# A decoder layer on one Trainium2 core: the final RMSNorm moved from channels-on-partitions to tokens-on-partitions, with the last down projection reordered

## The chip, the cores and the metric

The kernel runs on one core of one Trainium2 chip. The metric is the device time of one execution in microseconds (us). The core has five engines with a program each: TensorE (PE in the profile, its weight loads PEld), VectorE (DVE), ScalarE (ACT), GpSimd (POOL), and SyncE (SP), which issues the DMAs. They meet at semaphores only.

## What is computed

One inference step of a hybrid causal decoder with one layer: 1024 prompt tokens and 8 sample tokens, each a row of 1024 channels (`D_MODEL`). The layer adds sparse attention with a conformer convolution, cross-attention, and a ConvFFN to the residual stream `x`. The last two statements are what this study is about:

```python
    up = rmsnorm(x, lw['norm_ffn']) @ lw['w_up']
    up_ext = jnp.concatenate([ffn_prev.astype(up.dtype), up], axis=1)
    g, val = jnp.split(causal_dwconv(up_ext, lw['ffn_dw'], lw['ffn_db']), 2, axis=-1)
    x = x + (jax.nn.silu(g) * val) @ lw['w_down']
...
def rmsnorm(x, g):
    xf = x.astype(jnp.float32)
    y = xf * lax.rsqrt(jnp.mean(xf * xf, -1, keepdims=True) + RMS_EPS)
    return (y * g.astype(jnp.float32)).astype(x.dtype)
...
    y_prompt = rmsnorm(yp, norm_final)
    y_sample = rmsnorm(ys, norm_final)
```

## The kernel before

The residual stream lies in SBUF as `xT`: channels on the 128 partitions, in 8 blocks (`KT` = 8), and the 1032 tokens (`T`) along the free axis, taken in three thirds of 344 columns (`CH`). Every product is made from three matmuls on high and low parts (`w_hi`, `w_lo`; `h_hi`, `h_lo`; `g_hi`, `g_lo`). The order of the work on each engine is written out by hand, with semaphore counts as the only link between engines.

The ConvFFN runs over 11 groups of hidden channels (`NG`). For each group PE makes the up projection of the next group (`up`) and then the down projection of this one (`down`): 24 units of 6 matmuls, one for each of 8 channel blocks `m` and 3 thirds `c`, with `c` inside. Each unit goes to one PSUM bank, and DVE adds it to `xT` (L1596). Semaphore `g_done` counts units, `res_c` counts the adds; PE may start a unit when the add that frees its bank is done.

The end of the program, after the last `down` (L2093), is the part that the change rewrites. Before the change it runs so:

- While the last down group runs, ACT squares each finished channel block of `xT` (`squares(3)`, L805), and DVE sums the squares over blocks into `n_rstd` (L1184, L1187), four blocks after the first 12 adds and four after the last.
- PE turns the last two up-projection columns (`upl`) by five transposes (L2097), for the small output `ffn_out`, and sums `n_rstd` over partitions by a matmul with ones (`norm_sum`, L1658).
- DVE and ACT make the reciprocal root for each of the three thirds (L1191, L1192, L814), and DVE writes the normalised `yT` in eight instructions (L1196).
- For each of nine token tiles (eight of 128 prompt tokens, one of the 8 sample tokens) PE makes eight 128x128 transposes of `yT` into a pair of PSUM banks (L2110), ACT copies one bank and DVE the other into the token-major buffer `y_tok` (L1169, L1618), and SP sends it out by one 512 KB DMA (L657). There are two `y_tok` buffers and two bank pairs.

A norm with tokens on partitions stands at the program's start too, on the input: ACT squares a row of 1024 with a running sum and takes the root (L768, L769), DVE takes the reciprocal and scales by it and by the gain, broadcast over partitions (L1219, L1224).

Of the kernel before, what the change touches and what calls it, by code (L numbers as in the profile page):

```python
# [20 lines left out]
ALU = mybir.AluOpType  # L21
# [3 lines left out]
P = 128  # L25
D = 1024
# [3 lines left out]
DB = 8  # L30
# [186 lines left out]
def build(nc, a, o):  # L217
# [27 lines left out]
    def sem(name):  # L245
        return ctx.enter_context(nc.semaphore(name))
# [184 lines left out]

    r = rz.again(out_at)
    fst = r.take("ffn_out", [2 * 2 * FT, 5, P])
    ytk = [r.take(f"y_tok{i}", [P, D]) for i in range(2)]
    yT = rh.again().take("yT", [P, KT, T])

# [53 lines left out]
    y_out = [sem(f"y_out{i}") for i in range(2)]  # L490

# [42 lines left out]
    def _(sp):  # L534
# [117 lines left out]

        for t in range(NB + 1):
            sp.wait_ge(yo_a, t + 1)
            sp.wait_ge(yo_d, t + 1)
            if t < NB:
                sp.dma_start(o["y_prompt"][0, t * P:(t + 1) * P, :], ytk[t % 2][:, :]).then_inc(y_out[t % 2], 16)  # L657
            else:
                sp.dma_start(o["y_sample"][:, 0, :], ytk[t % 2][0:DB, :]).then_inc(y_out[t % 2], 16)
        sp.wait_ge(y_out[0], 16 * 5)  # L660
        sp.wait_ge(y_out[1], 16 * 4)
        sp.wait_ge(ffn_out, 16 * (2 + DB))
# [96 lines left out]
    def _(act):  # L759
# [47 lines left out]
        def norm(i):  # L807

            if i < 3:
                squares(i)  # L810
# [351 lines left out]

        norm(3)
        for t in range(NB + 1):
            act.wait_ge(yo_t, 2 * t + 1)
            if t >= 2:
                act.wait_ge(y_out[t % 2], 16 * (t // 2))
            rows = P if t < NB else DB
            act.activation(ytk[t % 2][0:rows, 0:512], ps[0:rows, 3 + 2 * (t % 2), :], ACT.Copy).then_inc(yo_a, 1)  # L1169


    @block.vector
    def _(dve):
        self_ = Chain(dve, dve_self)

        def norm(i, gain, residual=None):
# [16 lines left out]
            dve.wait_ge(n_rstd, 3 * i)  # L1193
            if i == 3:
                for k in range(KT):
                    dve.scalar_tensor_tensor(out=yT[:, k, :], in0=xT[:, k, :], scalar=vec[:, gain + k:gain + k + 1],  # L1196
                                             in1=nr[:, :], op0=ALU.mult, op1=ALU.mult).then_inc(n_h, 1)
                return
            for k in range(KT):
# [411 lines left out]
        self_.n = n0 + 4 * (NG - 1)  # L1611
        norm(3, 32, lambda k: down(NG - 1, k // 4, UNITS_TO[SLOTS - 2]) if k % 4 == 0 else None)
        for t in range(NB + 1):
            dve.wait_ge(yo_t, 2 * t + 2)
            if t >= 2:
                dve.wait_ge(y_out[t % 2], 16 * (t // 2))
            rows = P if t < NB else DB
            dve.tensor_copy(ytk[t % 2][0:rows, 512:1024], ps[0:rows, 4 + 2 * (t % 2), :]).then_inc(yo_d, 1)  # L1618


    @block.tensor
    def _(pe):
# [470 lines left out]
        down(NG - 1, SLOTS - 2, (NG - 1) % 2, True)  # L2093
# [50 lines left out]
```

## Time and profile before

| | |
|---|---|
| median of 3 timed runs | 1976.29 us (1969.69 to 1976.4) |
| profiled execution, its own time | 1968.74 us |
| span of that execution, first to last instruction | 1966.9 us |
| PE busy / DVE busy / ACT busy / POOL busy | 85% / 59% / 31% / 28% of the span |
| mean granted TensorE clock | 0.914 of full speed |

The profile and all rows below are of the one profiled execution, which took 1968.74 us; 1.84 us of that lie outside its span. Two of the three timed runs are about 7.6 us above it, one is 1 us above it. A busy share is an average over stages; the end of the program is read by its own windows.

### The profile page before, as it was taken

Reading aid. Unit: us, or ns where it says so; the run is one execution under the profiler, and the core shown is the slowest. Engines: PE = TensorE matmul, PEld = TensorE weight load, DVE = VectorE, ACT = ScalarE, POOL = GpSimd, SP = SyncE. Lnnn points to the kernel's source line nnn. Section 1 sums busy time; section 2 is a strip of 40 time slices with the busy share of each in tenths; the row PEclk is TensorE's granted clock in tenths of the full one; section 3 lists DMA queues with packets and bytes.
Section 4 is the critical chain, followed back from the end, with each engine's and each line's share of the span. In section 5 each row is a group of like instructions: output and inputs, shape, how many; then the busy total and the mean of one; then the engine's idle time right before and its main releaser. Section 6 shows DMA issues by size and latency. Waiting matters only on the chain.

```text
span 1966.9 us, 28667 instructions
## 1 busy us (share of the span) xinstructions
PE 1668.8 (85%) x10229; PEld 1506.3 (77%) x10229; DVE 1158.0 (59%) x2001; ACT 606.9 (31%) x1235; POOL 547.7 (28%) x342
## 2 busy tenths in 40 slices
PE   6978696997898387799788699999999999999983
PEld 6966595995373155599677599989989999999983
DVE  5467898999975465524633746336346336336366
ACT  6344555311221464401341332202212202212212
POOL 1231232222000254323001153433433433433420
PEclk9999798997688599999886899999999999999996
DMA  7320021321442100041012011111111111111102
GB/s 228 84 58 24 22 75 56 85 75 25 121 146 86 64 1 1 1 140 32 11 40 78 22 54 43 44 44 43 44 44 43 44 44 43 44 44 44 43 15 91
DMA packets 138747, 110.63 MB, mean 56 GB/s; under 512 B 12324, under 2 KB 120092, under 8 KB 138354
## 3 DMA queue, kind: packets, MB, share of 16 engines
q1 hardware_dynamic: 128325, 102.19, 17.3%
q10 hardware_dynamic: 10301, 6.73, 1.1%
q8 instruction: 87, 1.43, 0.3%
q14 instruction: 34, 0.28, 0.0%
HBM read 93.56 MB, written 16.00 MB: 56 GB/s over the span
## 4 chain that ended last, share of the span: by engine, by line
PE 67%; DVE 16%; issue 7%; ACT 5%; DMA 2%; POOL 1%; SPq 1%; DVEq 1%; ACTq 0%; POOLq 0%
PE ps L1634 40%; PE ps L1688 10%; PE ps L1626 4%; DVE hits L1326 2%; PE ps L1649 2%; PE ps L1944 2%; PE ps L1893 2%; PE ps L1867 1%; DVE logits L1495 1%; DVE up_conv L1578 1%; DVE n_rstd L1192 1%; DVE sc L1285 1%; DVE n_rstd L1187 1%; DVE up_conv L1577 1%; DVE logits L1492 1%
## 5 line engine op out<-in xcount | busy, mean ns | idle before, releaser
L1634 PE MATMUL ps<-h_hi,w_hi 128*128 128x344 f32 x1200 | 385.1, 321 | 8.7 <-DVE xT L1596 4.6
L681 POOL TENSOR_SCALAR w_hi<-w_raw 128x1024 fp32r<-128x1024 f32 (+1 forms) x107 | 118.3, 1106 | 973.3 <-PE ps L1634 508.0
L1634 PE MATMUL ps<-h_lo,w_hi 128*128 128x344 f32 x1200 | 384.0, 320 | 0.0
L1634 PE MATMUL ps<-h_hi,w_lo 128*128 128x344 f32 x1200 | 383.9, 320 | 0.0
L683 POOL TENSOR_TENSOR w_lo<-w_raw,w_hi 128x1024 fp32r<-128x1024 f32 (+1 forms) x107 | 283.6, 2650 | 8.9
L1634 PEld LDWEIGHTS ps<-h_hi,w_hi 128*128 128x128 f32 x1200 | 225.9, 188 | 10.3 <-DVE xT L1596 5.7
L1577 DVE SCALAR_TENSOR_TENSOR up_conv<-up,fw,up_conv 128x1024 f32<-128x1024 f32 x44 | 72.9, 1657 | 263.7 <-ACT upl L1142 263.7
L1634 PEld LDWEIGHTS ps<-h_hi,w_lo 128*128 128x128 f32 x1200 | 226.1, 188 | 0.0
L1634 PEld LDWEIGHTS ps<-h_lo,w_hi 128*128 128x128 f32 x1200 | 226.0, 188 | 0.0
L1596 DVE TENSOR_TENSOR xT<-xT,ps 128x344 f32<-128x344 f32 x264 | 135.2, 512 | 147.4 <-PE ps L1634 144.2
L1634 PE MATMUL ps<-g_hi,w_hi 128*128 128x344 f32 x528 | 175.5, 332 | 36.1 <-DVE xT L1596 36.1
L1688 PE MATMUL ps<-h_hi,w_hi 128*128 128x344 f32 (+1 forms) x600 | 198.9, 331 | 2.9 <-ACTq L869 2.9
L1688 PE MATMUL ps<-h_lo,w_hi 128*128 128x344 f32 (+1 forms) x600 | 195.0, 325 | 0.0
L1688 PE MATMUL ps<-h_hi,w_lo 128*128 128x344 f32 (+1 forms) x600 | 194.9, 325 | 0.0
L1634 PE MATMUL ps<-g_lo,w_hi 128*128 128x344 f32 x528 | 174.4, 330 | 0.0
L1634 PE MATMUL ps<-g_hi,w_lo 128*128 128x344 f32 x528 | 174.0, 330 | 0.0
L1139 ACT ACTIVATE up<-ps 128x344 f32<-128x344 f32 x132 | 61.8, 468 | 350.0 <-POOL g_lo L754 238.6
L1399 DVE SCALAR_TENSOR_TENSOR ps<-u,cw,ps 128x512 f32<-128x512 f32 x232 | 153.2, 747 | 0.2 <-issue 0.2
L1634 PEld LDWEIGHTS ps<-g_hi,w_hi 128*128 128x128 f32 x528 | 104.1, 197 | 39.5 <-DVE xT L1596 38.5
L1688 PEld LDWEIGHTS ps<-h_hi,w_hi 128*128 128x128 f32 (+1 forms) x600 | 115.1, 192 | 9.4 <-issue 7.8
L1688 PEld LDWEIGHTS ps<-h_lo,w_hi 128*128 128x128 f32 (+1 forms) x600 | 114.8, 191 | 0.8
L1688 PEld LDWEIGHTS ps<-h_hi,w_lo 128*128 128x128 f32 (+1 forms) x600 | 114.5, 191 | 0.4
(338 smaller groups left out, 2900.2 us busy)
## 6 DMA issues: line engine op xcount, KB each, us to landing
w_raw<-in_w_up SPq DMA_DIRECT2D x44, 512.0 KB, 3.9
w_raw<-in_w_in SPq DMA_DIRECT2D x24, 512.0 KB, 3.9
w_raw<-in_w_down SPq DMA_DIRECT2D x22, 512.0 KB, 3.6
s_k_page<-in_cache_k SPq DMA_DIRECT2D x32, 256.0 KB, 2.8
s_v_pages<-in_cache_v SPq DMA_DIRECT2D x32, 256.0 KB, 2.9
xT<-x_spill SPq DMA_DIRECT2D x1, 4128.0 KB, 12.2
x_tok<-in_x_prompt SPq DMA_DIRECT2D x8, 512.0 KB, 7.8
x_spill<-x_raw SPq DMA_DIRECT2D x16, 256.0 KB, 2.8
```

The source lines that it names most:

```text
L681: pool.tensor_scalar(view(wh), view(wr), 1.0, 0.0, ALU.mult, ALU.add).then_inc(w_hi, 1)
L683: pool.tensor_tensor(view(wl), view(wr), view(wh).bitcast(F32), ALU.subtract).then_inc(w_lo, 1)
L1139: act.activation(e[:, 2 + c * CH:2 + (c + 1) * CH], src, ACT.Copy)
L1326: dve.tensor_scalar(hit(b), row(b), col(cand, b), col(below, b), ALU.is_lt, ALU.add, accum_out=col(cnt, b)).then_inc(th_cnt, 1)
L1399: dve.scalar_tensor_tensor(out=ps[:, 4 + e, :], in0=u[:, m, bass.ds(j + 512 * e, 512)], scalar=cw[:, bass.ds(CT * j + m, 1)], in1=ps[:, 4 ...
L1577: dve.scalar_tensor_tensor(out=y_[:, 0:S], in0=e[:, 1:1 + S], scalar=w(1), in1=y_[:, 0:S], op0=ALU.mult, op1=ALU.add)
L1596: dve.tensor_tensor(xT[:, m, cols], xT[:, m, cols], ps[:, DOWN_BANKS[n % 5], 0:CH], ALU.add).then_inc(res_c, 1)
L1626: return pe.transpose(out, in_, ident[q:q + n, q:q + n])
L1634: mm = pe.matmul(out, view(w)[:, k, m0:m0 + m], x(k), start=(k == 0 and q == 0), stop=(k == ktiles - 1 and q == 2))
L1649: mm = pe.matmul(ps[:, 3 * e + c, 0:CH], w8(w, j)[:, k, :], x[:, k, at], start=(k == 0 and q == 0), stop=(k == KT - 1 and q == 2))
L1688: mm = pe.matmul(out, w8(w, js)[:, k, 0:cols], x[:, k, :], start=(k == 0 and q == 0), stop=(k == KT - 1 and q == 2))
L1893: mm = pe.matmul(ps[0:64, 2, :], spT[:, (b * NPG + q) * 64:(b * NPG + q + 1) * 64], vpg[b % 4][:, q, :], start=False, stop=(b == DB - 1 an ...
```

## The change

The norm is taken after the transposes instead of before. PE transposes the un-normalised `xT` of one token tile into two neighbouring PSUM banks; ACT reads both as one row of 1024, squares it with a running sum (into the dead buffer `y_squares`) and takes the root; DVE takes the reciprocal of 128x1 and scales the two banks by it and by the gain (`gain_final`, broadcast to all partitions by a new 512 KB DMA) straight into `y_tok`. The sums over blocks, the matmul with ones, the reciprocals over 1032 columns and `yT` are gone. There are four `y_tok` buffers, and three bank pairs at 3, 5 and 1.

The last down group goes by thirds of tokens (`LAST_DOWN`): the first two thirds for blocks 0 to 3, then for blocks 4 to 7, then the third third for all blocks. After 12 adds the first 256 tokens are complete, after 16 the first 640. So PE makes the transposes of tile 0 behind unit 17, tile 1 behind 19, tile 2 behind 21, and the others behind unit 23 (`OUT_BEHIND`); DVE scales tiles 0 and 1 behind adds 19 and 21 and the rest behind add 23 (`SCALED_BEHIND`). The sample tile is sixth of the nine. The last group uses four banks, not five. The `upl` transposes now stand ahead of the last group. Two small things go along: loads of the cross-attention cache reuse earlier semaphores, and POOL sets one more 128x1 constant.

```diff
+LAST_DOWN = ([(m, c) for h in range(2) for c in range(2) for m in range(4 * h, 4 * h + 4)] + [(m, 2) for m in range(KT)])
+LAST_BANKS = (0, 1, 2, 7)
+OUT_TILES = (0, 1, 2, 3, 4, NB, 5, 6, 7)
+OUT_BANK = (3, 5, 3, 5, 3, 5, 1, 3, 5)
+OUT_BEHIND = {18: (0,), 20: (1,), 22: (2,), 24: (3, 4, 5, 6, 7, 8)}
+SCALED_BEHIND = {20: (0,), 22: (1,), 24: (2, 3, 4, 5, 6, 7, 8)}
...
          sp.dma_start(o["ffn_sample"][0, :, 0, :], A["cache_ffn"][0, :, 1, :]).then_inc(ffn_out, 16)
+        sp.wait_ge(g_done, UNITS_TO[SLOTS - 4])
+        sp.dma_start(gfin[:, :], broadcast("norm_final")).then_inc(gain_in, 16)
...
-        for t in range(NB + 1):
-            sp.wait_ge(yo_a, t + 1)
-            sp.wait_ge(yo_d, t + 1)
+        for i, t in enumerate(OUT_TILES):
+            sp.wait_ge(yo_d, i + 1)
...
 -        squares(3)
...
-        norm(3)
-        for t in range(NB + 1):
-            act.wait_ge(yo_t, 2 * t + 1)
-            if t >= 2:
-                act.wait_ge(y_out[t % 2], 16 * (t // 2))
+        act.wait_ge(const_ok, 3)
+        for i, t in enumerate(OUT_TILES):
             rows = P if t < NB else DB
-            act.activation(ytk[t % 2][0:rows, 0:512], ps[0:rows, 3 + 2 * (t % 2), :], ACT.Copy).then_inc(yo_a, 1)
+            act.wait_ge(yo_t, i + 1)
+            self_.link(act.activation(ysq[0:rows, :], ps[0:rows, OUT_BANK[i]:OUT_BANK[i] + 2, :].rearrange("p a n -> p (a n)"), ACT.Square,
+                                      accum_out=ssf[0:rows, t:t + 1]))
+            act.activation(ssf[0:rows, t:t + 1], ssf[0:rows, t:t + 1], ACT.Sqrt, scale=1.0 / D, bias=epf[0:rows, :]).then_inc(yo_a, 1)
...
 -        norm(3, 32, lambda k: down(NG - 1, k // 4, UNITS_TO[SLOTS - 2]) if k % 4 == 0 else None)
-        for t in range(NB + 1):
-            dve.wait_ge(yo_t, 2 * t + 2)
-            if t >= 2:
-                dve.wait_ge(y_out[t % 2], 16 * (t // 2))
-            rows = P if t < NB else DB
-            dve.tensor_copy(ytk[t % 2][0:rows, 512:1024], ps[0:rows, 4 + 2 * (t % 2), :]).then_inc(yo_d, 1)
+        def out_tile(i):
+            t = OUT_TILES[i]
+            rows = P if t < NB else DB
+            dve.wait_ge(yo_a, i + 1)
+            dve.reciprocal(ssf[0:rows, t:t + 1], ssf[0:rows, t:t + 1]).then_inc(rstd_ok, 1)
+            dve.wait_ge(rstd_ok, NB + 3 + i + 1)
+            if i >= 4:
+                dve.wait_ge(y_out[i % 4], 16 * (i // 4))
+            dve.scalar_tensor_tensor(out=ytk[i % 4][0:rows, :], in0=ps[0:rows, OUT_BANK[i]:OUT_BANK[i] + 2, :].rearrange("p a n -> p (a n)"),
+                                     scalar=ssf[0:rows, t:t + 1], in1=gfin[0:rows, :], op0=ALU.mult, op1=ALU.mult).then_inc(yo_d, 1)
+
+        dve.wait_ge(gain_in, 48)
+        for n in range(25):
+            for i in SCALED_BEHIND.get(n, ()):
+                out_tile(i)
+            if n < 24:
...
+                dve.tensor_tensor(xT[:, m, cols], xT[:, m, cols], ps[:, LAST_BANKS[n % 4], 0:CH], ALU.add).then_inc(res_c, 1)
...
 -        down(NG - 1, SLOTS - 2, (NG - 1) % 2, True)
-
         pe.wait_ge(f_c, 6 + 12 * NG)
         for q in range(5):
             mm = tr(ps[0:88, 3 + q // 4, q % 4 * P:(q % 4 + 1) * P], upl[:, 2 * q:2 * q + 2, :].rearrange("p r c -> p (r c)"))
...
-        norm_sum(3)
-        pe.wait_ge(fo_c, 2)
-        pe.wait_ge(n_h, 3 * KT)
...
+            bank = OUT_BANK[i]
+            pe.wait_ge(res_c, RES_AT[3] + (12 if t < 2 else 16 if t < 5 else 24))
+            if i == 0:
+                pe.wait_ge(fo_c, 2)
+            if bank in OUT_BANK[:i]:
+                pe.wait_ge(yo_d, i - OUT_BANK[:i][::-1].index(bank))
...
+        for n in range(25):
+            for i in OUT_BEHIND.get(n, ()):
+                out_tile(i)
+            if n < 24:
...
+                pe.wait_ge(res_c, RES_AT[3] + max(n - 3, 0))
+                gemm(ps[:, LAST_BANKS[n % 4], 0:CH], SLOTS - 2 + m // 4, m % 4 * P, P, 2, lambda k: gh[e][:, k, at], lambda k: gl[e][:, k, at], 512).then_inc(g_done, 1)
```

In the order of instructions this shows at three places. First PE, from the last matmul of the last down group (`g_hi`, `w_lo`) on, before (`xT`, `yT` are the residual stream and its normalised copy, both with channels on partitions; in brackets the semaphores waited for):

```order
L1634 MATMUL ps<-g_hi_216,w_lo_67 128x344
L1626 MATMUL ps<-ident,upl 88x128 [waits f_c]
L1626 MATMUL ps<-ident,upl 88x128 x4
L1658 MATMUL ps<-n_rstd,ones 128x344 [waits n_acc]
L1658 MATMUL ps<-n_rstd,ones 128x344 x2
L1626 MATMUL ps<-ident,yT 128x128 [waits n_h,fo_c]
L1626 MATMUL ps<-ident,yT 128x128 x15
L1626 MATMUL ps<-ident,yT 128x128 [waits yo_d,yo_a]
L1626 MATMUL ps<-ident,yT 128x128 x7
L1626 MATMUL ps<-ident,yT 128x128 [waits yo_d,yo_a]
L1626 MATMUL ps<-ident,yT 128x128 x7
```

and in the changed kernel, from the same matmul on:

```order
L1651 MATMUL ps<-g_hi_216,w_lo_67 128x344
L1643 MATMUL ps<-ident,xT 128x128 [waits yo_d,res_c]
L1643 MATMUL ps<-ident,xT 128x128 x7
L1643 MATMUL ps<-ident,xT 128x128 [waits yo_d,res_c]
L1643 MATMUL ps<-ident,xT 128x128 x7
L1643 MATMUL ps<-ident,xT 8x128 [waits yo_d,res_c]
L1643 MATMUL ps<-ident,xT 8x128 x7
L1643 MATMUL ps<-ident,xT 128x128 [waits res_c]
L1643 MATMUL ps<-ident,xT 128x128 x7
L1643 MATMUL ps<-ident,xT 128x128 [waits yo_d,res_c]
L1643 MATMUL ps<-ident,xT 128x128 x7
```

The transposes read `xT`, not `yT`; the `upl` transposes and the matmul with ones no longer stand between the last unit and the tiles, three tiles have moved ahead of it, and a tile waits for `yo_d` (DVE's scaling) of the tile that had its banks.

Second DVE, from the second dozen of the last adds on, before (`n_sq` are ACT's squares, `n_rstd` their sum and its reciprocal root):

```order
L1596 TENSOR_TENSOR xT<-xT,ps 128x344 [waits res_c,g_done] x12
L1187 TENSOR_TENSOR n_rstd<-n_rstd,n_sq_91 128x1032 [waits n_acc,n_sq]
L1187 TENSOR_TENSOR n_rstd<-n_rstd,n_sq_92 128x1032 [waits n_acc,n_sq]
L1187 TENSOR_TENSOR n_rstd<-n_rstd,n_sq_91 128x1032 [waits n_acc,n_sq]
L1187 TENSOR_TENSOR n_rstd<-n_rstd,n_sq_92 128x1032 [waits n_acc,n_sq]
L1191 TENSOR_SCALAR n_rstd<-ps 128x344 [waits n_ss]
L1192 RECIPROCAL n_rstd<-n_rstd 128x344 [waits dve_self]
L1191 TENSOR_SCALAR n_rstd<-ps 128x344 [waits n_ss]
L1192 RECIPROCAL n_rstd<-n_rstd 128x344 [waits dve_self]
L1191 TENSOR_SCALAR n_rstd<-ps 128x344 [waits n_ss]
L1192 RECIPROCAL n_rstd<-n_rstd 128x344 [waits dve_self]
L1196 SCALAR_TENSOR_TENSOR yT<-xT,vec,n_rstd 128x1032 [waits n_rstd]
```

and in the changed kernel, from the first of the last 24 adds on (`y_ss` is the sum of squares of each token and then its root, `y_tok_223` to `226` the four output buffers):

```order
L1635 TENSOR_TENSOR xT<-xT,ps 128x344 [waits res_c,g_done,gain_in]
L1635 TENSOR_TENSOR xT<-xT,ps 128x344 [waits res_c,g_done] x19
L1619 RECIPROCAL y_ss<-y_ss 128x1 [waits yo_a]
L1623 SCALAR_TENSOR_TENSOR y_tok_223<-ps,y_ss,gain_final 128x1024 [waits rstd_ok]
L1635 TENSOR_TENSOR xT<-xT,ps 128x344 [waits res_c,g_done] x2
L1619 RECIPROCAL y_ss<-y_ss 128x1 [waits yo_a]
L1623 SCALAR_TENSOR_TENSOR y_tok_224<-ps,y_ss,gain_final 128x1024 [waits rstd_ok]
L1635 TENSOR_TENSOR xT<-xT,ps 128x344 [waits res_c,g_done] x2
L1619 RECIPROCAL y_ss<-y_ss 128x1 [waits yo_a]
L1623 SCALAR_TENSOR_TENSOR y_tok_225<-ps,y_ss,gain_final 128x1024 [waits rstd_ok]
L1619 RECIPROCAL y_ss<-y_ss 128x1 [waits yo_a]
L1623 SCALAR_TENSOR_TENSOR y_tok_226<-ps,y_ss,gain_final 128x1024 [waits rstd_ok]
```

The sums, the three reciprocals of 344 columns and the eight rows of `yT` are gone; a pair of a 128x1 reciprocal and one scaling stands for each tile, two pairs among the adds, and the first add waits for the gain.

Third ACT at the end, before:

```order
L805 ACTIVATE n_sq_92<-xT 128x1032 [waits res_c,n_acc]
L1161 ACTIVATE ffn_out<-ps 88x512 [waits fo_t]
L1161 ACTIVATE ffn_out<-ps 88x128 [waits fo_t]
L814 ACT_TABLE_LOAD
L814 ACTIVATE n_rstd<-n_rstd 128x344 [waits n_var] x3
L1169 ACTIVATE y_tok_221<-ps 128x512 [waits yo_t]
L1169 ACTIVATE y_tok_222<-ps 128x512 [waits yo_t]
```

and in the changed kernel:

```order
L1168 ACTIVATE ffn_out<-ps 88x512 [waits fo_t]
L1168 ACTIVATE ffn_out<-ps 88x128 [waits fo_t]
L1174 ACTIVATE y_squares,y_ss<-ps 128x1024 [waits yo_t,const_ok]
L1176 ACT_TABLE_LOAD
L1176 ACTIVATE y_ss<-y_ss,eps_final 128x1 [waits act_self]
L1174 ACTIVATE y_squares,y_ss<-ps 128x1024 [waits yo_t]
L1176 ACTIVATE y_ss<-y_ss,eps_final 128x1 [waits act_self]
```

The squares of `xT` and the copies out of PSUM are gone; a Square over 1024 columns of PSUM and a Sqrt of 128x1 stand for each tile, with one table load, ahead of the first Sqrt.

## Rows read from the trace of the kernel before

**Rows 1.** The page's first line: the profiled execution.
```profile
span 1966.9 us, 28667 instructions
```

**Rows 2.** Windows of the last 70 us (columns in the first row).
```profile
core 0: us, PE busy (x) PEld busy (x) DVE busy (x) ACT busy (x) POOL busy (x), PEclk, DMA share, GB/s
...
1896.47:1920.62 24.15, 23.24 (x146) 22.92 (x147) 16.02 (x27) 6.41 (x6) 2.82 (x2) 1.00 0.00 1
1920.62:1926.37 5.75, 0.54 (x6) 0.28 (x4) 5.35 (x5) 3.75 (x5) 0.00 (x0) 0.88 0.01 3
1926.37:1936.70 10.33, 3.80 (x6) 1.84 (x6) 8.16 (x6) 1.77 (x4) 0.00 (x0) 0.50 0.07 20
1936.70:1946.60 9.90, 0.00 (x0) 0.02 (x1) 9.72 (x8) 0.01 (x1) 0.00 (x0) 0.50 0.00 0
1946.60:1966.90 20.30, 11.61 (x72) 10.25 (x72) 6.21 (x9) 5.37 (x9) 0.00 (x0) 0.75 0.52 209
```

**Rows 3.** Chain that ended last: start us, us, engine or DMA, line.
```profile
1936.74 9.73 DVE yT L1196 x8
...
1946.61 1.96 PE ps L1626 x8
...
1952.86 2.62 DMA out_y_prompt<-y_tok
...
1959.80 4.00 DMA out_y_prompt<-y_tok
```

**Rows 4.** Timeline, last down group: start us, us, engine, line, [idle before <-releaser].
```profile
1898.63 0.51 DVE L1596 TENSOR_TENSOR xT<-xT,ps 128x344 f32<-128x344 f32 x1 [0.43 <-PE ps L1634]
...
1908.10 0.51 DVE L1596 TENSOR_TENSOR xT<-xT,ps 128x344 f32<-128x344 f32 x1 [0.43 <-PE ps L1634]
...
1920.64 0.51 DVE L1596 TENSOR_TENSOR xT<-xT,ps 128x344 f32<-128x344 f32 x1 [0.43 <-PE ps L1634]
...
1896.47 0.40 PE L1634 MATMUL ps<-g_hi,w_hi 128*128 128x344 f32 x1 [0.79 <-DVE xT L1596]
...
1913.70 0.43 PE L1634 MATMUL ps<-g_hi,w_hi 128*128 128x344 f32 x1 [0.91 <-DVE xT L1596]
```

**Rows 5.** Timeline, PE's transposes at the end.
```profile
1920.44 0.71 PE L1626 MATMUL ps<-ident,upl 128*88 128x128 f32 x5
...
1956.40 1.06 PE L1626 MATMUL ps<-ident,yT 128*128 128x128 f32 x8 [0.70 <-DVE y_tok L1618]
```

**Rows 6.** Timeline, ACT in the token norm at the program's start.
```profile
7.19 1.28 ACT L769 ACT_TABLE_LOAD   x1
8.48 0.29 ACT L769 ACTIVATE ss<-ss,eps 128x1 f32<-128x1 f32 x1
8.68 1.04 ACT L768 ACTIVATE sq_junk<-x_tok 128x1024 f32<-128x1024 f32 x1
...
9.85 0.29 ACT L769 ACTIVATE ss<-ss,eps 128x1 f32<-128x1 f32 x1
```

**Rows 7.** Timeline, DVE in the same token norm.
```profile
8.81 0.16 DVE L1219 RECIPROCAL ss<-ss 128x1 f32<-128x1 f32 x1 [8.81 <-ACT ss L769]
9.01 1.28 DVE L1224 SCALAR_TENSOR_TENSOR x_norm<-x_tok,ss,gain_mix 128x1024 f32<-128x1024 f32 x1
...
19.15 2.54 DVE L1224 SCALAR_TENSOR_TENSOR x_norm<-x_tok,ss,gain_mix 128x1024 f32<-128x1024 f32 x1
```

**Rows 8.** Groups by shape that read PSUM: xcount | busy us, mean ns.
```profile
L963 ACT ACTIVATE rr<-ps 128x512 f32<-128x512 f32 x48 | 28.2, 598 | 24.3 <-DVE sc L1285 12.3 <-PE ps L1782 9.8 <-DVE sc L1282 1.5
...
L1399 DVE SCALAR_TENSOR_TENSOR ps<-u,cw,ps 128x512 f32<-128x512 f32 x232 | 153.2, 747 | 0.2 <-issue 0.2
```

**Rows 9.** DMA issues (KB each, median us to landing) and two of SP's issues.
```profile
out_y_prompt<-y_tok SPq DMA_DIRECT2D x8, 512.0 KB, 2.6
...
gain_mix<-in_norm_mix SPq DMA_DIRECT2D x1, 512.0 KB, 6.5
...
1870.06 0.79 SPq L645 DMA_DIRECT2D out_ffn_sample<-in_cache_ffn  x1
...
1964.63 0.30 SPq L659 DMA_DIRECT2D out_y_sample<-y_tok  x1
```

**Rows 10.** Windows, while the output tiles leave.
```profile
1953.00:1955.00 2.00, 1.36 (x13) 1.15 (x13) 0.69 (x1) 0.60 (x1) 0.00 (x0) 1.00 0.73 299
```

More of the change, by code:

```diff
@@ L430, in build @@
     gl = [r.take(f"g_lo{i}", [P, 2, T], F32R) for i in range(2)]
[L432 to L435, printed above, removed]
+    fst = rz.again(out_at).take("ffn_out", [2 * 2 * FT, 5, P])
+    r = rh.again()
+    gfin = r.take("gain_final", [P, D])
+    ysq = r.take("y_squares", [P, D])
+    ytk = [r.take(f"y_tok{i}", [P, D]) for i in range(4)]
+    epf = rc.take("eps_final", [P, 1])
+    ssf = rc.take("y_ss", [P, NB + 1])
     x_spill = nc.dram_tensor("x_spill", [P, KT * T], F32).ap()
@@ L489, in build @@
     fo_t, fo_c, ffn_out, yo_t, yo_a, yo_d = (sem(x) for x in ("fo_t", "fo_c", "ffn_out_sem", "yo_t", "yo_a", "yo_d"))
-    y_out = [sem(f"y_out{i}") for i in range(2)]
+    y_out = [sem(f"y_out{i}") for i in range(4)]
     def x_arrived(eng, t):
@@ L807, in norm @@
         def norm(i):
-            if i < 3:
-                squares(i)
+            squares(i)
             for c in range(3):
@@ L1156, in _ @@
             up(2 * i + 2, 0)
-        squares(3)
         for q in range(2):
@@ L1193, in norm @@
             dve.wait_ge(n_rstd, 3 * i)
[L1194 to L1198, printed above, removed]
             for k in range(KT):
@@ L1611, in _ @@
         self_.n = n0 + 4 * (NG - 1)
[L1612 to L1618 removed]
+        def out_tile(i):
+            t = OUT_TILES[i]
+            rows = P if t < NB else DB
+            dve.wait_ge(yo_a, i + 1)
[10 more added lines that the diff above has]
+            if n < 24:
+                m, c = LAST_DOWN[n]
+                cols = slice(c * CH, (c + 1) * CH)
+                dve.wait_ge(g_done, UNITS_TO[SLOTS - 2] + n + 1)
+                dve.wait_ge(res_c, 6 + 48 + 24 * (NG - 1) + n)
+                dve.tensor_tensor(xT[:, m, cols], xT[:, m, cols], ps[:, LAST_BANKS[n % 4], 0:CH], ALU.add).then_inc(res_c, 1)
     @block.tensor
@@ L2070, in up, with down @@
                     gemm(ps[:, 3 * (q % 2) + c, 0:CH], SLOT_F + q, 0, P, KT, lambda k: hh[:, k, at], lambda k: hl[:, k, at]).then_inc(g_done, 1)
-        def down(g, slot0, e, last=False):
-            pe.wait_ge(f_c, 12 * g + (18 if last else 27))
+        def down(g, slot0, e):
+            pe.wait_ge(f_c, 12 * g + 27)
             pe.wait_ge(glo, 2 * g + 2)
@@ L2092, in _ @@
                 down(g, 6 * g + (SLOT_F + 8), e)
-        down(NG - 1, SLOTS - 2, (NG - 1) % 2, True)
         pe.wait_ge(f_c, 6 + 12 * NG)
@@ L2099, in _, with out_tile @@
                 mm.then_inc(fo_t, 1)
-        norm_sum(3)
-        pe.wait_ge(fo_c, 2)
-        pe.wait_ge(n_h, 3 * KT)
-        for t in range(NB + 1):
+        def out_tile(i):
+            t = OUT_TILES[i]
             cols = slice(t * P, (t + 1) * P) if t < NB else slice(S, T)
             rows = P if t < NB else DB
-            if t >= 2:
-                pe.wait_ge(yo_a, t - 1)
-                pe.wait_ge(yo_d, t - 1)
-            for k in range(KT):
-                mm = tr(ps[0:rows, 3 + 2 * (t % 2) + k // 4, k % 4 * P:(k % 4 + 1) * P], yT[:, k, cols])
-                if k % 4 == 3:
-                    mm.then_inc(yo_t, 1)
+            bank = OUT_BANK[i]
[4 more added lines that the diff above has]
+                pe.wait_ge(yo_d, i - OUT_BANK[:i][::-1].index(bank))
+            for k in range(KT):
+                mm = tr(ps[0:rows, bank + k // 4, k % 4 * P:(k % 4 + 1) * P], xT[:, k, cols])
+            mm.then_inc(yo_t, 1)
+        e = (NG - 1) % 2
+        pe.wait_ge(glo, 2 * NG)
+        for n in range(25):
+            for i in OUT_BEHIND.get(n, ()):
+                out_tile(i)
+            if n < 24:
+                m, c = LAST_DOWN[n]
+                at = slice(c * CH, (c + 1) * CH)
+                pe.wait_ge(w_lo, SLOTS - 1 + m // 4)
+                pe.wait_ge(res_c, RES_AT[3] + max(n - 3, 0))
+                gemm(ps[:, LAST_BANKS[n % 4], 0:CH], SLOTS - 2 + m // 4, m % 4 * P, P, 2, lambda k: gh[e][:, k, at], lambda k: gl[e][:, k, at], 512).then_inc(g_done, 1)
     ctx.close()
```

19 lines of the change are left out of this document (9 added, 10 removed).

## The prediction

> **What bounds the kernel now.** The page's first line gives the span, 1966.9 us [rows 1]. The change touches only the program's end, so I next read that end by windows, stage for stage [rows 2], and there look at PE's column first. In the last down group, 1896.47 to 1920.62, PE is busy 23.24 of 24.15 us at the full clock (2.4 GHz): it is the bound there. From 1920.62 to 1966.9, 46.3 us, it has almost nothing to do in the first three windows: DVE is busy 5.35 of 5.75, 8.16 of 10.33 and 9.72 of 9.90 us. These are the sums of squares, the reciprocals over 1032 columns and `yT`. In the last window no engine is the bound; the chain of waits names output DMAs there, 2.62 us and 4.00 us [rows 3]. With two `y_tok` buffers a copy waits until the DMA from two tiles before has landed. So the end of the program is a series: sums, then reciprocals, then `yT` (9.73 us), then tiles at the pace of DMA landings. Nothing in it overlaps with PE's group but four of the sums.
>
> **The change, part by part.** I lay a schedule from the start of the last group and count to the end, all times on the axis of the span.
>
> *Start.* PE waits 0.79 us at 1896.47 for DVE's last add of the group before [rows 4], and waits for the same add after the change. The five `upl` transposes take 0.71 us [rows 5] and fit into this wait. I cost them at nothing; if they do not fit they cost 0.7 us.
>
> *The group.* Adds 1 to 11 run from 1898.63 to 1908.10, 0.947 us each, which is PE's pace for a unit [rows 4]. Add 23 would be 22 x 0.947 after 1898.63, at 1919.46. It started at 1920.64: DVE's sums held it up, and PE stood 0.91 us at 1913.70 for an add [rows 4]. Without them 1.2 us come back. In their place come three sets of eight transposes, 1.06 us each [rows 5], 3.2 us in all. Add 23 then starts at 1922.64 and ends at 1923.15. DVE's scalings of tiles 0 and 1 also stand among the adds, but behind add 19, and the last unit waits for add 19 only, so they hold up no unit. The four banks instead of five are no cost either: an add takes 0.51 us and a unit 0.947, so DVE is never more than a unit behind.
>
> *A tile.* PE: eight transposes, 1.06 us. ACT: at the program's start Square to the end of Sqrt is 8.68 to 10.14, 1.46 us [rows 6]. That Square read SBUF; the new one reads PSUM. An ACT read of 128x512 from PSUM takes 0.598 us [rows 8], two of them 1.20, against 1.04 for the Square, so 1.46 to 1.62; I take 1.46, since one instruction of 1024 pays its start once. DVE: from the reciprocal's start to the scaling's end 8.81 to 10.29, 1.48 us [rows 7]. With a PSUM operand twice 0.747 [rows 8] is 1.49 against 1.28, so 1.48 to 1.69; I take 1.48, for the row differs in one operand only. No row has a Square or a scaling over two banks.
>
> The Trainium skill, page "VectorE: DVE Perf Modes", section "The TRN2 errata", gives VectorE 120 cycles at 0.96 GHz beside one per element from PSUM, where SBUF has 58; by it the scaling would be an estimated 1.19 us, below the row, and the sum about 0.6 us shorter. The row is kept.
>
> *The tail.* PE, ACT and DVE work on different tiles; a tile's banks come free when DVE has scaled it. By position in the order (0 to 8; the sample tile is 5):
>
> - 2: transposed before the last units. DVE is free at 1923.15, done 1924.63.
> - 3: PE 1922.6 to 1923.7, ACT to 1925.15, DVE to 1926.63.
> - 4: waits for the banks of 2. PE to 1925.7, ACT to 1927.15, DVE to 1928.63.
> - 5: waits for the banks of 3. PE to 1927.7, ACT to 1929.15, DVE to 1930.63.
> - 6: banks 1 and 2 are free. PE to 1928.75, ACT behind 5 to 1930.6, DVE to 1932.1.
> - 7: PE to 1929.8, ACT to 1932.05, DVE to 1933.6.
> - 8: PE to 1931.7, ACT to 1933.5, DVE to 1935.1.
>
> So a tile costs some 1.7 us on average, first by the loop through two bank pairs, then by ACT and DVE. With three tiles ahead, six remain, and none waits for an output DMA: position 4 is the first to use a buffer again, and the DMA of position 0 went out about 8 us before.
>
> *The end.* The last full tile goes out at 1935.15. A `y_prompt` DMA lands 2.6 us after its issue in the median, and took 4.00 once on the chain [rows 3, 9]; tiles now follow each other every 1.5 us. While they left at 299 GB/s the DMA engines were 0.73 busy [rows 10], so 512 KB need about 524/(299/0.73) = 1.28 us of all engines: it fits, closely. From the last, small, DMA's issue at 1964.63 to the end of the span were 2.3 us [rows 9]. For 512 KB I take 3.2 us, between 2.3 and 4.6 (4.00 and a little for the last wait): end at 1938.3.
>
> *What costs nothing.* The gain's DMA is issued behind one at 1870.06 and such a load landed in 6.5 us [rows 9], so near 1878, 20 us ahead of the first add; if it came after 1897.7 it would hold every add. SP's wait for `g_done` stands behind all weight loads, and the DMAs behind it wait for later things. The table load, 1.28 us [rows 6], is now at tile 0, whose scaling stands behind two more units, 1.9 us: hidden, and if not, DVE loses a few tenths. `ffn_out` leaves 20 us sooner. The changed semaphores and the 128x1 constant do no work on a path.
>
> *Sum.* 1966.9 - 1938.3 = 28.6 us saved: the profiled 1968.74 would become 1940.1. Of the runs shown two of three lie near the median, 1976.29, 7.6 us above this execution, and no row tells why. The forecast is for the median: 1976.3 - 28.6 = 1947.7 us.
>
> **Rivals.**
>
> *Half clock in the tail.* PE is busy only some 60% of the time in the tail. Before, with PE idle, the granted clock was 0.50 (1.2 GHz) from 1926.37 to 1946.6 [rows 2], and eight transposes then took 1.96 us [rows 3]; when tiles ran one every 1.7 us it was 1.00 [rows 10], with the same eight transposes in each, which speaks against it. At 1.96 the loop through the banks is 0.9 us longer; two rounds of it: 1.9 us, 1949.6.
>
> *DVE slowed.* One scaling took 2.54 us instead of 1.28 at the program's start [rows 7]. Seven such in the tail would be bound by DVE alone: 1923.15 + 7 x 2.74 = 1942.3 in place of 1935.1, 7.2 us later, 1954.9. POOL, which was busy in the early part, does nothing in the tail [rows 2], and this speaks against it.
>
> *The early tiles bring nothing.* If tile 0's scaling came late and PE stood for its banks, the three early sets would be dead weight: three scalings more in the tail, 3 x 1.48 = 4.4 us, 1952.1. Tile 2 needs tile 0's banks: PE is there after two units, a set and two units more (1919.4) and the scaling of tile 0 should end at 1919, so there is little slack.
>
> *Table loads at every tile.* ACT goes from Square to Sqrt and back nine times. If each change loaded a table, a tile would cost ACT 2 x 1.28 more: near 1.37 (a Square's start to where the next could start) + 2.56 = 3.93 us. Nine of them from the end of tile 0's transposes (1914.6) end at 1950.0, with scaling and DMA 1954.7: 12.2 us saved, 1964.1. Against it: at the start one load stands ahead of the first Sqrt and none at the next Square or Sqrt, 8.68 and 9.85 [rows 6]. The Trainium skill, page "ScalarE: Activation LUTs", section "Table sets: the hidden batching unit", says to batch calls by set, and this loop does the reverse, unless both functions are in one set; by this trace they are.
>
> *Slower: no overlap between tiles.* If every tile had to wait until the one before had landed, a tile would cost 1.06 + 1.46 + 1.48 + 2.6 = 6.6 us. Position 2 would land at 1927.2, six more at 1966.8, the end at 1967.3; at half clock (1.96) at 1972.7, 5.8 us later than before, 1982. It decides from 6.5 us for each tile. For it speaks that the tiles before were bound by landings; against it, that PE now waits for `yo_d`, not for a DMA, and that there are four buffers.
>
> **How the numbers follow.** Forecast 0.80; half clock 0.06; DVE slowed 0.06; early tiles in vain 0.03; table loads 0.03; no overlap 0.02. The unknown prices beside the forecast: ACT 0.5 (0.16 on three tiles), DVE 1.5 (0.21 x 7), the last landing -0.9 to +1.4, `upl` 0.7; so 24 to 30 us saved. From the profiled execution's time the low end is 1968.7 - 30 = 1939, from the highest run the other is 1976.4 - 22 = 1954, which takes in half clock and the early tiles. I give 1938 to 1954. A measurement of this kernel tells about 0.5% (10 us) from no change. All cases but the last are faster by more than that: 0.97 faster, 0.02 same, 0.01 slower.
>
> **What would show it.** Right: the five `upl` transposes at about 1895.8; add 23 at 1922 to 1923; three sets of transposes among the last units with no wait of PE over 0.3 us; DVE scalings of about 1.3 us each, seven of them from 1923 to 1935; one table load; the clock at 1.00 to 1932; the last output DMA issued near 1935. Wrong: a scaling over 1.5 or a Square over 1.3 us; PE standing among the last units; output DMAs that land later than 5 us; or a change of the time before 1896, where nothing should move.

## The result

The change made the kernel faster: median 1950.24 us of 4 runs (1943.79 to 1957.16), against 1975.62 us for before in 4 runs (1969.69 to 1976.4). The ratio is 0.9864, with a 95% interval of 0.9835 to 0.9893. The forecast was 1947.7 us. The profiled execution of the changed kernel took 1949.85 us, and its page begins so (compare [rows 1]):

```profile
span 1948.0 us, 28640 instructions
```

The spans of the two profiled executions differ by 18.9 us only, less than the 28.6 forecast. The windows of the changed kernel, cut at the first matmul of the last down group, say why (columns as in [rows 2]):

```profile
0.00:1907.18 1907.18, 1646.46 (x10008) 1485.62 (x10008) 1110.71 (x1946) 589.93 (x1213) 545.05 (x342) 0.91 0.19 56
1907.18:1933.60 26.42, 26.41 (x176) 26.06 (x176) 15.24 (x30) 5.94 (x12) 2.83 (x2) 1.00 0.11 40
...
1936.00:1938.00 2.00, 1.27 (x12) 1.14 (x13) 1.17 (x3) 1.51 (x4) 0.00 (x0) 1.00 0.71 281
...
1940.00:1942.00 2.00, 1.14 (x9) 0.85 (x8) 1.97 (x3) 1.85 (x7) 0.00 (x0) 1.00 0.62 227
1942.00:1944.00 2.00, 0.00 (x0) 0.00 (x0) 1.93 (x5) 1.38 (x3) 0.00 (x0) 0.76 0.52 215
```

The last group began at 1907.18 instead of 1896.47 [rows 2], 10.7 us later, though the change moves nothing ahead of it but five small transposes, the gain's DMA, a constant and the semaphores of some loads. From that matmul to the end of the span ("the last stretch" from here on) there are 40.8 us instead of 70.5: 29.7 us saved. So the change did what it was to do in its own stretch, and two executions differ by some 10 us ahead of it. Experiments 1 and 2 ask whether these 10 us belong to the change.

In the group's window PE is now busy 26.41 of 26.42 us: the units, the three early tiles and the first tile behind them leave it no gap. The timeline of PE in the changed kernel:

```profile
1906.23 0.71 PE L1643 MATMUL ps<-ident,upl 128*88 128x128 f32 x5
1907.18 0.40 PE L1651 MATMUL ps<-g_hi,w_hi 128*128 128x344 f32 x1 [0.24 <-DVE xT L1598]
...
1929.79 1.04 PE L1643 MATMUL ps<-ident,xT 128*128 128x128 f32 x8
1930.58 0.40 PE L1651 MATMUL ps<-g_hi,w_hi 128*128 128x344 f32 x1
...
1934.80 1.06 PE L1643 MATMUL ps<-ident,xT 128*128 128x128 f32 x8 [1.22 <-DVE y_tok L1623]
```

The `upl` transposes fit into the wait ahead of the group: of 0.79 us [rows 4], 0.24 are left. Position 2's transposes at 1929.79 wait for nothing. From position 4 on (1934.80) PE waits for DVE's scalings, which free the banks. DVE's timeline, from the first scaling on:

```profile
1928.12 0.16 DVE L1619 RECIPROCAL y_ss<-y_ss 128x1 f32<-128x1 f32 x1 [0.41 <-ACT y_ss L1176]
1928.32 1.28 DVE L1623 SCALAR_TENSOR_TENSOR y_tok<-ps,y_ss,gain_final 128x1024 f32<-128x1024 f32 x1
...
1932.75 0.52 DVE L1635 TENSOR_TENSOR xT<-xT,ps 128x344 f32<-128x344 f32 x1 [0.29 <-PE ps L1651]
...
1935.30 1.28 DVE L1623 SCALAR_TENSOR_TENSOR y_tok<-ps,y_ss,gain_final 128x1024 f32<-128x1024 f32 x1
1937.38 0.16 DVE L1619 RECIPROCAL y_ss<-y_ss 128x1 f32<-128x1 f32 x1 [0.80 <-ACT y_ss L1176]
1937.58 1.28 DVE L1623 SCALAR_TENSOR_TENSOR y_tok<-ps,y_ss,gain_final 128x1024 f32<-128x1024 f32 x1
...
1943.64 1.28 DVE L1623 SCALAR_TENSOR_TENSOR y_tok<-ps,y_ss,gain_final 128x1024 f32<-128x1024 f32 x1
```

And ACT's, for positions 0 and 1:

```profile
1925.37 1.03 ACT L1174 ACTIVATE y_squares<-ps 128x1024 f32<-128x1024 f32 x1 [17.74 <-PE ps L1643]
1926.29 0.19 ACT L1174 ACTIVATION_READ_ACCUMULATOR y_squares<-ps 128x1 f32 x1
1926.50 1.28 ACT L1176 ACT_TABLE_LOAD   x1
1927.79 0.30 ACT L1176 ACTIVATE y_ss<-y_ss,eps_final 128x1 f32<-128x1 f32 x1
1928.07 1.03 ACT L1174 ACTIVATE y_squares<-ps 128x1024 f32<-128x1024 f32 x1
...
1929.22 0.29 ACT L1176 ACTIVATE y_ss<-y_ss,eps_final 128x1 f32<-128x1 f32 x1
```

The one table load stands ahead of the first root and delays the first scaling: DVE waits 0.41 us for it at 1928.12. After it a tile costs ACT 1.44 us and DVE 1.48, and DVE's later waits (0.80 at 1937.38) are for the next tile's root.

The chain that ended last, behind the last unit (start, us, what), shows what sets the end now; it answers to [rows 3]:

```profile
1933.62 1.12 ACT y_squares L1174 x2
...
1935.30 1.30 DVE y_tok L1623
...
1936.73 1.05 PE ps L1643 x8
1937.80 1.11 ACT y_squares L1174 x2
...
1939.45 1.17 DVE y_tok L1623
...
1943.64 1.28 DVE y_tok L1623
```

First it runs round the loop ACT, DVE, PE, ACT, DVE, since a tile in the same banks can begin only when DVE has scaled the one before; from 1939.45 on it is DVE alone, a tile every 1.4 us. No output DMA stands on it but the last.

### The profile page after: what moved, and what is told of

It reads as the page before. It is cut to its first block, busy times and chain, and to the rows that moved or that the text cites. A ratio compares the mean times of both kernels' runs of the same rounds, so it can differ in the third digit from the quotient of the medians.

```text
span 1948.0 us, 28640 instructions
## 1 busy us (share of the span) xinstructions
PE 1678.0 (86%) x10223; PEld 1515.8 (78%) x10223; DVE 1135.4 (58%) x1988; ACT 604.1 (31%) x1242; POOL 547.9 (28%) x343
## 4 chain that ended last, share of the span: by engine, by line
PE 68%; DVE 15%; issue 7%; ACT 5%; DMA 2%; SPq 1%; POOL 1%; DVEq 1%; ACTq 0%; POOLq 0%
PE ps L1651 41%; PE ps L1705 10%; PE ps L1643 4%; DVE hits L1328 2%; PE ps L1666 2%; PE ps L1961 2%; PE ps L1884 1%; DVE logits L1497 1%; DVE up_conv L1580 1%; PE ps L1910 1%; DVE sc L1287 1%; DVE up_conv L1579 1%; DVE logits L1494 1%; PE ps L1862 1%; PE ps L1847 1%
## 5 line engine op out<-in xcount | busy, mean ns | idle before, releaser
L1598 DVE TENSOR_TENSOR xT<-xT,ps 128x344 f32<-128x344 f32 x240 | 122.9, 512 | 146.6 <-PE ps L1651 144.5
```

The lines of the kernel that those rows point to most:

```text
L1598: dve.tensor_tensor(xT[:, m, cols], xT[:, m, cols], ps[:, DOWN_BANKS[n % 5], 0:CH], ALU.add).then_inc(res_c, 1)
```

## The experiments

The executions scatter ahead of the last group by more than most parts of the change are worth, so each kernel is judged by its last stretch: first matmul of the last group to the end of the span, in one profiled execution of each. The start is on the axis of the span; the next two columns and the last are counted from it, the fifth from the last scaling.

| kernel | start of the group | add 23 starts | last scaling (or copy) ends | end behind it | last stretch |
|---|---|---|---|---|---|
| before | 1896.47 | 24.18 | 68.09 | 2.39 | 70.48 |
| before again (1) | 1902.77 | 24.17 | 68.53 | 2.28 | 70.81 |
| changed | 1907.18 | 25.57 | 37.74 | 3.07 | 40.81 |
| changed again (2) | 1897.49 | 25.58 | 37.76 | 3.07 | 40.83 |
| before, four buffers (3) | 1905.71 | 24.17 | 62.41 | 5.12 | 67.53 |
| norm alone (4) | 1906.27 | 22.97 | 45.07 | 3.06 | 48.13 |
| no early tiles (5) | 1908.71 | 22.97 | 43.91 | 3.08 | 46.99 |
| two buffers (6) | 1902.38 | 25.61 | 42.08 | 3.06 | 45.14 |
| three bank pairs (7) | 1892.29 | 25.57 | 36.39 | 3.07 | 39.46 |
| five early tiles (8) | 1903.99 | 27.34 | 36.11 | 3.08 | 39.19 |
| sample tile last (9) | 1892.88 | 27.32 | 36.12 | 2.21 | 38.33 |

**1 and 2. Are the 10.7 us ahead of the group the change's?** Before was run again unchanged, and later the changed kernel too.

> The kernel before, unchanged, profiled a second time. The last stretch, from the first matmul of the last down group to the end of the span, took 70.4 us in the first profile of before and 40.8 us in the changed kernel, so 29.6 us less; but the spans differ by 18.9 us, because the last down group began 10.7 us later (1907.2 against 1896.5). Theory: the 10.7 us are the scatter of executions (the granted clock in the stages ahead), so that here the last group begins anywhere from 1896 to 1907 and the last stretch is again 70.4 us, within 0.5. Rival: the change slows the stages ahead of the last group (a shared semaphore, the added constant), and the last group of before begins again within 1 us of 1896.5.

> The changed kernel, unchanged, on the same chip as the run with the sample tile last. Theory: its last stretch is again 40.8 us, within 0.5; its last group begins anywhere from 1892 to 1909 us, as in the other runs; the ratio to before is 0.985 to 0.988. Rival: the begin of the last group is 1907 again, within 1 us, as if the change had moved it.

Before's last group now began at 1902.77 and took 1975.45 us in all (before beside it 1980.07); the changed kernel's now began at 1897.49, 9.7 us earlier than in its first profile. The windows ahead of the group, of before again and then of the changed kernel again:

```profile
0.00:1902.77 1902.77, 1636.51 (x10002) 1478.29 (x10003) 1110.20 (x1946) 589.20 (x1212) 543.65 (x341) 0.91 0.19 56
```

```profile
0.00:1897.49 1897.49, 1636.00 (x10008) 1477.67 (x10008) 1109.49 (x1946) 589.46 (x1213) 543.63 (x342) 0.92 0.19 56
```

What matters in these rows is PE's busy time at the same count of matmuls: 1646.46 us in the changed kernel's first execution and 1636.00 in the second, 10.5 apart, while DVE, ACT and POOL move by 1.4 us at most. The same 10,008 matmuls took longer where the granted clock was lower (0.91 against 0.92). So the start scatters for either kernel (1892 to 1909 in the table), mostly with the clock (PE was busy 1627.55 us ahead of the group in the execution where it began earliest, experiment 7, and 1644.90 in the latest, experiment 5), and the last stretch repeats within 0.4 us (before) and 0.02 us (changed). Not wholly with it: five early tiles (8) had 1635.66 us of PE ahead of the group, as little as the changed kernel again, and began 6.5 us later than that; what else moved it is not known. In six runs the changed kernel had a median of 1945.96 us, before on the same chip 1977.79; ratio 0.9847 (0.9815 to 0.988), just below the expected 0.985.

**3. The buffers alone.** Before with four `y_tok` buffers (the new ones in SBUF that is free by then):

```diff
-    ytk = [r.take(f"y_tok{i}", [P, D]) for i in range(2)]
+    ytk = [r.take(f"y_tok{i}", [P, D]) for i in range(4)]
...
-            if t >= 2:
-                act.wait_ge(y_out[t % 2], 16 * (t // 2))
+            if t >= 4:
+                act.wait_ge(y_out[t % 4], 16 * (t // 4))
```

> The kernel before with four output buffers instead of two, and nothing else of the change but the shared semaphores. Theory: the tiles at the end are then bound by PE's transposes at half clock and by the DMA's rate (512 KB in 1.3 us), and the last stretch falls from 70.4 to 65.5 us (64 to 67). Rival: DMA landings already follow each other as fast as they can, 1.74 us for each tile, and the last stretch stays at 69 to 70.5 us.

The stretch is 67.53 us, 3.0 less than before, half a microsecond above the expected range. The tiles' copies end 5.7 us earlier, but the span ends 5.12 us after the last of them instead of 2.39. The windows of that end:

```profile
1964.00:1966.00 2.00, 2.00 (x19) 1.78 (x18) 1.44 (x3) 1.20 (x2) 0.00 (x0) 1.00 0.99 404
1966.00:1968.00 2.00, 1.23 (x12) 0.78 (x10) 1.27 (x3) 1.17 (x2) 0.00 (x0) 1.00 1.02 395
1968.00:1970.00 2.00, 0.00 (x0) 0.00 (x0) 0.11 (x1) 0.01 (x1) 0.00 (x0) 1.00 1.02 406
```

With the waits gone and PE back at the full clock, a tile comes about every 1.0 us (last five copies), and the DMA engines, fully busy at some 400 GB/s, become the bound: what the buffers give, the transfers take half of back. The run itself took 1975.03 us.

**4. The norm alone.** The changed kernel with all tiles behind the group and two buffers, so that the new norm is left as the main change:

```diff
-OUT_BEHIND = {18: (0,), 20: (1,), 22: (2,), 24: (3, 4, 5, 6, 7, 8)}
-SCALED_BEHIND = {20: (0,), 22: (1,), 24: (2, 3, 4, 5, 6, 7, 8)}
+OUT_BEHIND = {24: (0, 1, 2, 3, 4, 5, 6, 7, 8)}
+SCALED_BEHIND = {24: (0, 1, 2, 3, 4, 5, 6, 7, 8)}
...
-            if i >= 4:
-                dve.wait_ge(y_out[i % 4], 16 * (i // 4))
+            if i >= 2:
+                dve.wait_ge(y_out[i % 2], 16 * (i // 2))
```

> The changed kernel with all nine tiles behind the last down group and with two output buffers: of the change only the norm with tokens on partitions is left. Theory: the norm alone brings most of the gain, since the sums, reciprocals and the normalised copy are gone whatever the buffers do; from the run without early tiles (47.0 us) only the last tile waits for a landing more, so the last stretch is 48.2 us (47 to 51) against 70.5 before. Rival: buffers and early tiles add up, 4.3 us for two buffers on top of 47.0, and more: 52 us or above.

48.13 us as expected (time 1956.2 us, before on the same chip 1974.9 in the median of 7). The norm on token partitions, with what goes along in this kernel (the `upl` transposes ahead of the group, the order by thirds, the sample tile sixth), saves 22.4 of the 29.7 us; early tiles and buffers together the other 7.3. The new order with the old norm was not tried, so those parts are not told apart.

**5. No early tiles,** four buffers (the first two pairs of lines above):

> The changed kernel, but all nine tiles stand behind unit 23 on PE and behind add 23 on DVE. Theory: three tiles fewer hide behind the last group; PE saves 2.6 us of transposes in the group and the tail has three tiles more, at about 2 us each by the loop through two bank pairs, and the table load comes into the open: the last stretch is 45 us (43.5 to 46.5) against 40.8. Rival: the early transposes cost PE what they save in the tail: 41 to 42 us.

46.99 us, above the expected range; the run took 1957.49 us. The windows of this kernel's tail show what was not in that expectation:

```profile
1934.00:1936.00 2.00, 0.00 (x0) 0.00 (x0) 0.60 (x2) 1.99 (x3) 0.00 (x0) 1.00 0.00 0
...
1938.00:1940.00 2.00, 2.00 (x11) 2.00 (x10) 0.24 (x1) 1.16 (x3) 0.00 (x0) 0.50 0.95 383
...
1944.00:1946.00 2.00, 2.00 (x11) 1.70 (x10) 1.45 (x2) 1.25 (x4) 0.00 (x0) 0.50 0.64 262
```

and its timeline, where the clock fell:

```profile
1931.48 1.91 PE L1643 MATMUL ps<-ident,xT 128*128 128x128 f32 x16
...
1933.74 1.28 ACT L1176 ACT_TABLE_LOAD   x1
...
1936.99 3.48 PE L1643 MATMUL ps<-ident,xT 128*128 128x128 f32 x16 [3.61 <-DVE y_tok L1623]
```

With no units behind it, the table load stands in the open, PE waits 3.61 us, and the granted clock then falls to 0.50 (1.2 GHz): two tiles' transposes take 3.48 us behind that wait and 1.91 ahead of it. "Half clock in the tail" does occur, in this kernel. In the changed one it does not: the windows above show 1.00 until 1942. So the early tiles are worth 6.2 us beside four buffers, part of it the clock.

**6. Two buffers,** early tiles kept (the last lines of the diff of 4):

> The changed kernel with two output buffers instead of four, so that a scaling waits until the output of two tiles before has landed. Theory: tiles come every 2 us in the first half of the tail and an output lands 2.7 us after its issue, so only the last three tiles wait, and the last stretch is 42.8 us (42 to 44) against 40.8. Rival: the buffers carry a large part of the gain, each pair of tiles costs a scaling and a landing one after the other as before the change, and the last stretch is 47 us or more.

45.14 us: 1.1 above the expected range and 1.9 below the rival's bound, so neither held; the run took 1949.31 us. Two pieces of its chain:

```profile
1934.13 4.92 DMA out_y_prompt<-y_tok
...
1940.46 2.63 DMA out_y_prompt<-y_tok
```

Position 4's output landed after 4.92 us instead of 2.63, and position 6 had to wait for its buffer: about 2.3 us, nearly the whole excess over the expected 42.8. So four buffers are worth 4.3 us here, of which half only because one transfer came late (below, on the hardware). As measured the parts do not add up: against the norm alone early tiles give 3.0 us, buffers 1.1, both 7.3. But the 3.0 holds that late landing, which experiment 4 did not have; without it early tiles alone would give an estimated 5.3, and the parts 6.4 of the 7.3. The 1.1 holds the second fall of the clock in experiment 5, where experiment 4 had only one. That the parts need each other is thus not shown.

**7. Three bank pairs from position 4 on.** Does the loop through two pairs bound the first half of the tail?

```diff
-OUT_BANK = (3, 5, 3, 5, 3, 5, 1, 3, 5)
+OUT_BANK = (3, 5, 3, 5, 1, 3, 5, 1, 3)
...
-            pe.wait_ge(res_c, RES_AT[3] + (12 if t < 2 else 16 if t < 5 else 24))
+            pe.wait_ge(res_c, RES_AT[3] + (24 if bank == 1 or t >= 5 else 12 if t < 2 else 16))
```

> The changed kernel with the tail's tiles going round three pairs of PSUM banks (5, 1, 3, 5, 1, 3 for positions 3 to 8) where it had two and one use of the third. Theory: in the first half of the tail the loop through a pair of banks (transposes, square and root, reciprocal and scaling, 4.1 us for two tiles) is the bound; with three pairs ACT and DVE are, at 1.4 us for each tile, so the last scaling ends 1.3 us sooner and the last stretch is 39.5 us (39 to 40) against 40.8. Rival: ACT and DVE were the bound throughout, and it stays at 40.6 to 41.0.

39.46 us, as expected, 1.35 less than the changed kernel. DVE's scalings of positions 3 and 4:

```profile
1920.41 1.28 DVE L1623 SCALAR_TENSOR_TENSOR y_tok<-ps,y_ss,gain_final 128x1024 f32<-128x1024 f32 x1
1921.61 0.15 DVE L1619 RECIPROCAL y_ss<-y_ss 128x1 f32<-128x1 f32 x1
1921.80 1.28 DVE L1623 SCALAR_TENSOR_TENSOR y_tok<-ps,y_ss,gain_final 128x1024 f32<-128x1024 f32 x1
```

They follow each other in 1.39 us, where the changed kernel had 2.28 (1935.30 and 1937.58 above). The loop was the bound there; with it gone DVE is, from position 3 to the end. The one run took 1933.54 us, but its group had begun at 1892.29, 14.9 us ahead of the changed kernel's profile: of that time only 1.35 us are the edit's.

**8. Five tiles ahead,** with the last group strictly by thirds (`c` outside, all eight `m` inside):

```diff
+LAST_DOWN = [(m, c) for c in range(3) for m in range(KT)]
+OUT_BANK = (3, 5, 3, 5, 3, 1, 5, 3, 1)
+OUT_BEHIND = {12: (0,), 14: (1,), 18: (2,), 20: (3,), 22: (4,), 24: (5, 6, 7, 8)}
+SCALED_BEHIND = {14: (0,), 16: (1,), 20: (2,), 22: (3,), 24: (4, 5, 6, 7, 8)}
```

> The changed kernel with the last down group by thirds of tokens alone (all eight blocks of the first third, then of the second, then of the third), five tiles among the units (behind units 11, 13, 17, 19 and 21) and the third pair of banks used for positions 5 and 8. Theory: two more tiles cost PE 0.87 us each in the group and save two passes of 1.4 to 2 us in the tail, so the last stretch is 38.3 us (37.5 to 39.3) against 40.8, and the time is about 0.1% below the changed kernel's, 1.4 to 1.6% below before, which this many runs tell from before but not from the changed kernel. Rival: DVE's scalings hold up the adds and PE stands among the units: 40.5 us or more.

39.19 us, 1.6 less than the changed kernel and within the range. Add 23 starts at 27.34, 1.77 later than with three early tiles: 0.88 us for each of the two more sets. Median 1944.38 us of 4 runs (1942.91 to 1946.64); ratio to before 0.9842 (0.9822 to 0.9861).

**9. The same, and the sample tile last,** so that the last output is 32 KB and not 512:

```diff
-OUT_TILES = (0, 1, 2, 3, 4, NB, 5, 6, 7)
+OUT_TILES = (0, 1, 2, 3, 4, 5, 6, 7, NB)
```

> The kernel with five early tiles, and the sample tile last instead of sixth, so that the last output is 32 KB and not 512 KB. Theory: what follows the last scaling is the landing of its own output; before the change, with the 32 KB output last, it was 2.3 to 2.4 us, and with a 512 KB output last 3.1 us, so the last stretch falls from 39.2 to 38.4 us (38.1 to 38.8), and the time stays about 0.1% below the changed kernel's. Rival: the last full tile, issued 1.4 us ahead, lands as late as before, and the stretch stays at 39.0 or more.

38.33 us, as expected: the end comes 2.21 us behind the last scaling instead of 3.08. Median 1941.28 us of 6 runs (1933.06 to 1947.74), ratio 0.9822 (0.979 to 0.9853), beside 1945.96 and 0.9847 for the changed kernel on the same chip. The intervals overlap; the time alone does not tell these two apart, the last stretch does, by 2.5 us. By the last stretch it is the best version tried.

## Why the prediction was right

The time fell into the range, 2.5 us above the forecast. That the median came so near is partly luck: the four runs spread over 13.4 us, and the medians of before and of the changed kernel differ by 25.4 us here and by 31.8 in experiment 2, on either side of the last stretch's 29.7. What the prediction can be judged by is that stretch, where 28.6 were forecast. By its steps, each counted from the first matmul of the last group:

- *Start.* Right: the `upl` transposes cost nothing, and no add waited for the gain.
- *The group.* Add 23 was put at 26.17 and came at 25.57. Without early tiles it comes at 22.97 (experiment 5), as the pace of units alone had it (22.99), so the term that was mis-sized is the set of transposes: 0.87 us among units (2.60 for three), not 1.06. The 1.06 of [rows 5] is a set that stands alone, from the first start to the last end; between units its ends overlap with its neighbours.
- *A tile.* ACT 1.44 us (1928.07 to 1929.51, the end of position 1's root), DVE 1.48 (1928.12 to 1929.60): as taken, from rows that read SBUF. A scaling from two banks took 1.28 us, as in [rows 7]. The Trainium skill, page "VectorE: DVE Perf Modes", section "The TRN2 errata", gave an estimated 1.19; the measurement stands, 0.09 above it.
- *The tail.* From add 23's start to the end of the last scaling 12.46 us were forecast and 12.17 measured. Its shape was right too: first the loop through two bank pairs (experiment 7), then DVE. Two small errors partly cancel in it: once round the loop took 4.15 us, from scaling to scaling in the same banks (1935.30 to 1939.45), where 4.00 were forecast with nothing for the hand-over between engines; and DVE alone took 1.40 a tile (1939.45 to 1943.64), not 1.48, since the next reciprocal begins before the scaling's shown end (1921.61 against 1920.41 + 1.28 in experiment 7).
- *The end.* 3.2 forecast, 3.07 measured.
- *The sum.* 0.60 + 0.29 + 0.13 are the 1.02 us by which the stretch is shorter than the 41.83 between 1896.47 and 1938.3.

One sign of a wrong forecast that the prediction named did appear, a change of the time before 1896: the group began 10.7 us later. Experiments 1 and 2 put it down to scatter that either kernel shows, mostly in the granted clock ahead of the group. What sets the clock in one execution and not in the next stays open.

The rivals: *half clock* not in the changed kernel, but in experiment 5 by a wait of PE. *DVE slowed*: no scaling above 1.29 us. *Early tiles in vain*: refuted, they are worth 6.2 us; but tile 0's scaling ended at 1929.60 and position 2's transposes began at 1929.79, so the slack was 0.2 us. *Table loads*: one load in the stretch, and Square followed Sqrt without another (1927.79 and 1928.07 above). It was not hidden wholly, since DVE waited 0.41 us at 1928.12; the adds behind it were late, and no unit was. The Trainium skill, page "ScalarE: Activation LUTs", section "Table sets: the hidden batching unit", asks to batch calls by set; the trace agrees in so far as both functions here run from one set. *No overlap*: refuted by the chain, where tiles follow every 1.4 us at the end.

## What to carry to other kernels

When a reduction has to cross partitions and the data is to be transposed anyway, take the reduction after the transpose: each tile then needs only its own data, and the end becomes a pipeline instead of a series (22.4 us here, with what goes along). Ask after each step what is the bound now: here it was the landings with two buffers, the loop through the banks with four, and DVE with a third pair of banks. And where executions scatter by more than the step is worth, compare the stretch from a mark in the program to its end, not the span.

## What the hardware showed unasked

Output DMAs of 512 KB mostly land in 2.6 or 2.7 us, before and after, but one, or two in a row, land late. Of the output line in the changed kernel the trace says:

```profile
DMA to landing us min/median/max: 2.6/2.7/4.4
```

The late one was issued at 1936.61. In the DMA queues of 1936 to 1942 there is one packet that no line of the program issues:

```profile
q8 instruction: 1, 0.02, 1.5%
```

A packet of the queue for instructions moves at that time, 0.02 MB in this view and 16,384 bytes in the trace's record of it. The same pair, one such packet and a late landing, stands in before (4.54 us for the tile issued at 1958.03), in before again (4.17), in two buffers (4.92) and in the changed kernel again (4.04). In the kernels of experiments 4 and 5 no such packet moved while outputs did, and no output whose landing the trace has took over 2.7 us. In experiments 7, 8 and 9 the packet moved too, and there the latest landing took only 3.6, 3.3 and 3.3 us, so it has no fixed price. With two buffers the late landing is on the chain, with four it costs nothing. That the packet is the cause was seen only as this coincidence and not tried. The Trainium skill, page "Runtime: NRT & Kernel Launch", section "Instruction fetch mechanics", says that an engine's instructions are refilled by DMA in blocks of 16 KiB; the size of the packet agrees, and the page tells of no cost to other transfers.

Two more. An accumulating Square shows a second instruction, ACTIVATION_READ_ACCUMULATOR, of 0.19 us (1926.29 above). And the granted clock stayed at 1.00 through the changed kernel's tail as long as PE had tiles (until 1942), where PE's longest wait between tiles was 1.22 us (1934.80), while in experiment 5 it fell to 0.50 behind a wait of 3.61 us and again from 1944 without such a wait just ahead; what made it fall the second time stays open.
